# A 64-expert MoE layer: from four ranked experts per iteration to 48 pairs of 64-place tiles

## The reference

```python
def _moe(x, w_router, router_bias, w_gu, w_down, w_sh_gu, w_sh_down):
    scores = jax.nn.sigmoid((xt @ w_router).astype(jnp.float32))
    _, sel = lax.top_k(scores + router_bias.astype(jnp.float32), TOP_K)
    s_sel = jnp.take_along_axis(scores, sel, axis=-1)
    g = s_sel / jnp.sum(s_sel, axis=-1, keepdims=True) * ROUTED_SCALE
    gates_t = ...                                # 0 where a token is not routed
    def add_expert(e, acc):
        h = xt @ w_gu[e]
        a = jax.nn.silu(h[:, :D_EXPERT]) * h[:, D_EXPERT:]
        return acc + (a * gates_t[e][:, None]) @ w_down[e]
    routed = lax.fori_loop(0, N_EXPERTS, add_expert, jnp.zeros_like(xt))
    ...                                          # plus a shared expert of the same size
```

## Time and profile before

| | us |
|---|---|
| median of 3 runs (1662.83, 1664.14, 1669.38) | 1664.14 |
| the profiled execution, its span | 1662.2 |
| expert stage, layer 0: first B matmul to the layer norm's first add | 181.99 to 822.39 |
| expert stage, layer 1 | 1003.76 to 1647.36 |
| PE busy | 1594.4 (96%) |
| DVE, ACT, POOL busy | 900.1, 757.8, 438.0 |

### The profile page before, as it was taken

How to read it: one execution, slowest core, us unless ns; L and a number is a source line. 1 busy time by engine, 2 the same in 40 slices (tenths; PEclk the granted TensorE clock), 3 DMA queues, 4 the chain that set the end, 5 groups by cost and what they waited for, 6 DMA issues and landing times.

```text
span 1662.2 us, 28154 instructions
## 1 busy us (share of the span) xinstructions
PE 1594.4 (96%) x9726; PEld 1206.1 (73%) x9726; DVE 900.1 (54%) x1397; ACT 757.8 (46%) x1023; POOL 438.0 (26%) x307
## 2 busy tenths in 40 slices
PE   7999999999999999999899989999999999999996
PEld 7888776776767776777588876777776777766763
DVE  1876555445455555555648654555555555555446
ACT  5674344444444444444257643444444444444442
POOL 6671112221111222112266611111222112121230
PEclk9999999999999999999999999999999999999998
DMA  9542899999999999999873449999999999999993
GB/s 317 163 148 82 337 378 362 382 375 385 366 370 368 380 371 370 369 376 369 306 240 105 127 153 348 377 364 383 367 385 367 371 365 380 368 379 373 372 364 143
DMA packets 132948, 536.26 MB, mean 323 GB/s; under 512 B 22780, under 2 KB 62248, under 8 KB 82984
## 3 DMA queue, kind: packets, MB, share of 16 engines
q1 hardware_dynamic: 105648, 454.00, 69.4%
q0 software_dynamic: 23136, 76.60, 17.2%
q10 hardware_dynamic: 4120, 5.07, 1.0%
HBM read 495.60 MB, written 40.02 MB: 322 GB/s over the span
## 4 chain that ended last, share of the span: by engine, by line
PE 64%; DMA 14%; DVE 9%; ACT 4%; issue 4%; DVEq 4%; POOL 1%; ACTq 0%; SPq 0%; POOLq 0%
PE ps L1168 11%; DMA raw<-in_w_exp_down_dram 10%; PE ps L1070 10%; PE ps L1230 6%; PE ps L1048 5%; PE ps L1049 5%; PE ps L1050 5%; PE ps L804 5%; PE ps L1194 4%; PE ps L1078 4%; DVEq L1964 3%; ACT w_hi L1532 3%; DVE raw_r L1901 2%; PE ps L964 2%; DMA raw<-in_w_exp_gu_dram 2%
## 5 line engine op out<-in xcount | busy, mean ns | idle before, releaser
L1901 DVE TENSOR_TENSOR raw_r<-raw,w_hi 128x2048 fp32r<-128x2048 f32 x192 | 439.0, 2291 | 473.9 <-ACT w_hi L1532 473.8
L1532 ACT CAST w_hi<-raw 128x2048 fp32r<-128x2048 f32 x192 | 365.4, 1906 | 364.0 <-DMA raw<-in_w_exp_down_dram 222.4
L1048 PE MATMUL ps<-x_hi,w_hi 128*128 128x256 f32 x1072 | 306.9, 286 | 0.0
L1049 PE MATMUL ps<-x_lo,w_hi 128*128 128x256 f32 x1072 | 305.2, 285 | 0.0
L1050 PE MATMUL ps<-x_hi,raw_r 128*128 128x256 f32 x1072 | 303.2, 283 | 0.0
L1194 PE MATMUL ps<-raw,xc 128*64 128x512 f32 x1024 | 233.8, 598 | 1.2 <-DMA raw<-in_w_exp_gu_dram 1.2
L1048 PEld LDWEIGHTS ps<-x_hi,w_hi 128*128 128x128 f32 x1072 | 210.9, 197 | 28.6 <-issue 26.7
L1049 PEld LDWEIGHTS ps<-x_lo,w_hi 128*128 128x128 f32 x1072 | 212.5, 198 | 0.9
L1050 PEld LDWEIGHTS ps<-x_hi,raw_r 128*128 128x128 f32 x1072 | 212.7, 198 | 0.0
L1194 PEld LDWEIGHTS ps<-raw,xc 128*64 128x64 f32 x1024 | 67.8, 136 | 118.9 <-issue 109.6
L760 POOL DMA_INDIRECT sums_by_token<-o_c,token_out_c x30 | 74.1, 2469 | 291.9 <-DMA sums_by_token<-o_b,token_out 271.9
(11 more groups left out here) (359 smaller groups left out, 2819.0 us busy)
## 6 DMA issues: line engine op xcount, KB each, us to landing
raw<-in_w_exp_gu_dram SPq DMA_DIRECT2D x256, 1024.0 KB, 9.4
raw<-in_w_exp_down_dram SPq DMA_DIRECT2D x128, 1024.0 KB, 7.8
raw<-in_w_in_dram SPq DMA_DIRECT2D x22, 1024.0 KB, 10.3
raw<-in_w_out_dram SPq DMA_DIRECT2D x8, 1024.0 KB, 5.2
sums_by_token<-zeros POOLq DMA_DIRECT2D x10, 512.0 KB, 6.6
raw<-in_w_sh_gu_dram SPq DMA_DIRECT2D x4, 1024.0 KB, 5.2
row_a<-gates_by_rank SPq DMA_DIRECT2D x32, 128.0 KB, 11.7
raw<-in_w_in_dram SPq DMA_DIRECT2D x2, 1040.0 KB, 12.4
```

Of the source, the lines that this page charges most:

```text
L1048: nc.tensor.matmul(o, h, x_hi[:, c, :], start=(first and i == 0), stop=False, skip_group_check=True)
L1049: nc.tensor.matmul(o, h, x_lo[:, c, :], start=False, stop=False, skip_group_check=True)
L1532: nc.scalar.copy(w_hi[CAST[j] % 3][:], raw[:, j % RING, 0:UNIT_F]).then_inc(hi_done, 1)
L1901: nc.vector.tensor_tensor(raw_r[:, s, 0:UNIT_F], raw[:, s, 0:UNIT_F], w_hi[CAST[j] % 3][:], ALU.subtract)\
```

## The change

The expert stage becomes 48 pairs per layer. A pair is two tiles of 64 places side by side in plain fp32, as C1 and C2 were. 32 "base" pairs hold experts 2m and 2m+1, in fixed order; 16 "over" pairs stand for what does not fit into an expert's first 64 places. The list goes base, base, over, and again. The two tiles of an over pair fetch their weights by row index, a row outside the table's bounds being skipped; which tiles are in use is worked out from the counts on the chip. All 16 over pairs run through PE whether they hold anything or not.

- **PE**: per pair 16 matmuls of gate/up (L1176), 8 of the pair before's down (L1199), two transposes (L1186). The split weights and three-fold matmuls of A and B are gone, with the casts on ACT and the subtractions on DVE.
- **POOL**: per pair four gathers of token quarters (L699, 128 rows of 1 KB each), a read of the 128 places' sums (L711), a write of them (L718), and in two pairs of three a fetch of two over tiles' weights (L740 gate/up or L749 down). The read for pair n waits until the sums of pair n-2 are stored; the write of pair n-1 waits for DVE's addition. There are four sum tables in DRAM (two by parity, two by half), cleared in each layer.
- **DVE**: per pair it turns the gathered tokens (L1825, 128x1024), multiplies silu, gate and up (L1833) and adds PE's result to the sums read (L1842, two of 128x512). The last two pairs are not written back but added by a one-hot matmul; then the tables are read and added.
- **SP**: base weights only, six units per base pair, into 12 units (the ring of six and six more); a load waits for the base pair before last.
- **Routing part**: the ranking is gone. Per token and expert a code (column and place) is worked out; two sets of 16 matmuls turn them into a token index and a gate per place, and one more spreads the index over the four quarters.
- **Program's start**: POOL no longer waits for rows of zeros to land before it goes on; some 50 small constants (`table_at`) are set there.

```diff
+    NBASE = NE // 2
+    NOVER = (SEQ * TOPK // HALF - 1 + 1) // 2
+    NPAIR = NBASE + NOVER
+    KINDS = [("base", 2 * i + r) if r < 2 else ("over", i) for i in range(NOVER) for r in range(3)]
...
-                def gather(it, first=False):
...
-                with pool.Fori(0, NIT - 1) as it:
-                    gather(it + 1)
-                    pool.wait_ge(o_b_ready, done(layer, o_b_ready, it + 1))
-                    pool.sem_inc(pool_turn, 1)
-                    pool.indirect_dma_start(added_rows, bass.IndirectOffsetOnAxis(ap=token_out[:, 0:1], axis=0), o_b[:], None,
-                                            compute_op=ALU.add).then_inc(o_b_added, 16)
...
+                def fetch_x(n):
+
+                    for g in range(PIECES):
+                        pool.indirect_dma_start(xg[n % 2][:, g, :], None, x_rows,
+                                                bass.IndirectOffsetOnAxis(ap=x_at[:, g, COLUMN[n]:COLUMN[n] + 1], axis=0),
+                                                bounds_check=SEQ * PIECES - 1, oob_is_err=False).then_inc(xg_loaded[n % 2], 16)
...
+                for n in range(NADD + 1):
+                    if n + 2 < NPAIR:
+                        pool.wait_ge(xt_ready, done(layer, xt_ready, n + 1))
+                        pool.sem_inc(pool_turn, 1)
+                        fetch_x(n + 2)
+                    if 2 <= n:
+                        sums_landed(n - 2)
+                    if 1 <= n < NADD:
+                        fetch_sums(n)
+                    if n % 3 == 0 and n // 3 < NOVER:
+                        fetch_gate_up(n // 3)
+                    elif n % 3 == 1 and n // 3 < NOVER:
+                        fetch_down(n // 3)
+                    if n == NADD:
+                        fetch_tables(0)
+                    if n >= 1:
+                        store_sums(n - 1)
...
+                def gate_up(n):
+
+                    pe.wait_ge(xt_ready, done(layer, xt_ready, n + 1))
+                    if n >= 2:
+                        pe.wait_ge(act_ready, done(layer, act_ready, n - 1))
...
+                            for h in range(2):
+                                last = nc.tensor.matmul(ps[lane(h), n % 2, :], xt[n % 2][:, c, 2 * h:2 * h + 2, :].rearrange("p g s -> p (g s)"),
+                                                        gu_unit(n, h, half)[:, i, :], start=(c == 0), stop=(c == KC - 1))
...
+                for n in range(NPAIR):
+                    gate_up(n)
+                    if n >= 1:
+                        down(n - 1)
+                    transpose_act(n)
...
+                def add_sums(n):
+
+                    dve.wait_ge(sums_here[n % 2], done(layer, sums_here[n % 2], 16 * (n // 2 + 1)))
+                    for half in range(2):
+                        part = sums[n % 2][:, half * 512:(half + 1) * 512]
+                        dve.wait_ge(down_ps, done(layer, down_ps, 2 * n + half + 1))
+                        last = nc.vector.tensor_tensor(part, part, ps[:, 2 + 2 * (n % 2) + half, :], ALU.add)
+                    last.then_inc(sums_added, 1)
```

More of the change, by code:

```diff
@@ L227, in build @@
[L227 to L232, removed]
+        unit = [raw[:, s, 0:UNIT_F] for s in range(RING)]
+        unit += [sb(f"unit{RING + s}", [P, UNIT_F], where=[shared_base + s * KB8])[:] for s in range(RING)]
@@ L1138, in _ @@
[L1138 to L1142 removed]
+                pe.wait_ge(token_in_ready, done(layer, token_in_ready, 1))
+                for i in range(NT * TOPK):
+                    last = nc.tensor.matmul(ps[:, 2, 0:NPAIR], at_place[:, i, :], token_in[:, i, :], start=(i == 0),
+                                            stop=(i == NT * TOPK - 1))
@@ L1144, in _ @@
+                for i in range(NT * TOPK):
+                    last = nc.tensor.matmul(ps[:, 3, 0:NPAIR], at_place[:, i, :], gate_in[:, i, :], start=(i == 0),
+                                            stop=(i == NT * TOPK - 1))
+                last.then_inc(gate_ps, 1)
                 pe.wait_ge(a_ready, done(layer, a_ready, 1))
@@ L1263, in _ @@
-                with pe.Fori(0, NIT - 1) as it:
-                    step(it, False)
-                step(NIT - 1, True)
+                            for h in range(2):
+                                last = nc.tensor.matmul(ps[lane(h), 2 + 2 * (n % 2) + half, :], at_c[n % 2][:, c, lane(h)],
+                                                        down_unit(n, h)[:, c, half * 512:(half + 1) * 512],
+                                                        start=(c == 0), stop=(c == FC - 1))
+                        last.then_inc(down_ps, 1)
@@ new lines, in _ @@
+                dve.drain()
+                for t in range(NT):
+                    part = slice(t * TOPK, (t + 1) * TOPK)
+                    last = nc.vector.tensor_scalar(token_in[:, part, :], in_col[:, part, :], token_neg[:, t:t + 1], None, ALU.mult)
+                last.then_inc(token_in_ready, 1)
+                shared_lo(2)
+                dve.wait_ge(token_ps, done(layer, token_ps, 1))
+                nc.vector.tensor_scalar(token_at[:], ps[:, 2, 0:NPAIR], float(FAR), None, ALU.add)
@@ new lines, in add_tables @@
+                def add_tables(parity, t):
+                    dve.wait_ge(table_loaded[parity][t], done(layer, table_loaded[parity][t], 32))
+                    for h in range(2):
+                        dve.drain()
+                        last = nc.vector.tensor_tensor(x_tok[:, t, :], x_tok[:, t, :], tables[2 * parity + h][:, t * D:(t + 1) * D], ALU.add)
+                    return last
+                over_rows()
+                transpose_x_of(0)
+                dve.wait_ge(gate_ps, done(layer, gate_ps, 1))
@@ new lines, in _ @@
+                nc.vector.tensor_copy(gate_at[:], ps[:, 3, 0:NPAIR])
+                dve.drain()
+                dve.wait_ge(unit_used, done(layer, unit_used, SH))
+                dve.wait_ge(x_perm_ready, done(layer, x_perm_ready, NT))
+                for t in range(NT):
+                    for half in range(2):
+                        part = x_tok[:, t, half * 512:(half + 1) * 512]
+                        last = nc.vector.scalar_tensor_tensor(part, part, ALPHA, ps[:, 4 + 2 * t + half, :], ALU.mult, ALU.add)
```

991 lines of the change are left out of this document (414 added, 577 removed).

## The result

The changed kernel takes 1715.17 us (1710.06 to 1717.55) against 1663.49 for the kernel before in the same series: 1.029 times as long, interval 1.027 to 1.032. The forecast was 1539, faster.

| us | before | after | difference | forecast |
|---|---|---|---|---|
| start of layer 0 to first gate/up | 181.99 | 202.33 | +20.3 | +12.5 |
| expert stage, layer 0 | 640.4 | 647.3 | +6.9 | -72 |
| its end to layer 1's first gate/up | 181.4 | 202.5 | +21.2 | +10.5 |
| expert stage, layer 1 | 643.6 | 647.3 | +3.7 | -76 |

The account below looks back on a forecast made before the run. It took the DMA engines to bound the expert stage, closely followed by PE and POOL's chain: 1662.2 + 2 + 2 x 10.5 + (568 - 640.4) + (568 - 643.6) = 1537, as median 1539 us; own range 1493 to 1591.

Parts of the forecast that it names:

- the third price of the stage: Expert stage: POOL's chain of landings and issues takes 31.1 to 35.7 us per three pairs, just below the DMA engines.
- 2L + 14.9: POOL's chain per three pairs: two write landings L, each 8.1 to 10.4 us, plus issues of 6.2 and 8.7 us.
- The first rival: Expert stage: POOL's chain sets the period; 1607 us at landings of 11.1, 1650 at 11.8; chance 0.16.
- The second loop: Expert stage: read landing, addition, write landing for every two pairs, 23.6 us against 22.4 of PE.
- the routing part: Before the first gate/up in each layer: the new path adds 10.5 us per layer, 7 to 14.
- PE: a pair's gate/up: Expert stage: gate/up 7.16 us, down 3.58, 11.18 per pair with transposes, 33.5 per three pairs.
- The DMA engines: 35.7 forecast: Expert stage: transfers per three pairs need 35.7 us, bounds 34.4 and 37.8, the later limit than PE.
- the 568 forecast: Expert stage of each layer: 560 us by the DMA engines plus 8 for close limits; range 545 to 594.
- The start: Program's start: POOL's 9.92 us wait for zeros goes, constants take about as long; +2 us, from -5 to +5.
- The next layer's first weights: Between layers: they wait for the tables' addition, covered by the layer norm; if not, 10 us once.
- An issue of the new kinds: POOL, expert stage: rival that issuing sets the period, slower than before above 1.77 us per issue with gap; chance 0.13.
- Memory: Expert stage: rival that memory gives only 358 GB/s, stage 618 us, kernel 1639 us; chance 0.05.

Follow-up runs that it names:

- e4: The changed kernel without the fetches of over weights, except the first pair's; PE still runs all over pairs: 1578.63 us (one run).
- e3: The changed kernel with two thirds of the base weights' bytes left out, one chunk of each unit standing for all: 1479.1 us (one run).
- e1: The changed kernel with POOL's list reordered, over fetch and write of sums ahead of the landing wait and the read of sums: 1718.29 us.
- e8: The changed kernel with PE's two waits in the routing part filled by 22 and 5 matmuls that nobody reads: 1699.34 us.
- e5: e2 with PE's two waits in the routing part filled by 22 and 10 matmuls that nobody reads: 1557.76 us.
- e2: The changed kernel with the write of sums accumulating in the transfer and no read of sums; DVE copies instead of adding: 1565.68 us.
- e7: e2 without the fetches of over weights, except the first pair's: 1560.57 us (one run).

## Why the prediction was wrong

*The step that failed is the third price of the stage, POOL's chain.* The prediction set it at 31.1 to 35.7 us per three pairs, "Below the DMA engines, if only just", and so priced the stage by the DMA engines. It is 40.6, where the DMA engines need about 36 (e4), and so it set the period. In the formula 2L + 14.9 both terms were too low. The two landings were put at 16.2 to 20.8; by the medians they are 23.0. One of them, 9.8, lies in the forecast range of 8.1 to 10.4. The other, 13.2, does not: its write is queued behind two skipped fetches, of which the prediction counted the issues alone, and without them it lands after 10.6 (e4). Half the rows and no accumulation did not save the 2.3 us that the lower bound took off 10.4: beside full DMA engines such writes land after 10.6 and 9.6 (e4). What does shorten a landing is less traffic beside it (e3). And the rest is 17.3, not 14.9: an issue is 1.30 with its gap, not 1.24, and POOL goes on 0.8 us after a landing.

*The first rival had it.* It was priced at 1607 us for L of 11.1 and 1650 for 11.8, with a chance of 0.16. With the measured landings and rest it gives 23.0 + 17.3 = 40.3, close to the 40.6 of the trace; 16 x 40.6 = 650 for the stage's 647. Its 11.1 was near the mean of the two landings, 11.5; of the 3.5 us per three pairs that its price lacked, 2.4 lie in the rest. The second loop that it mentions, read, addition, write, is no footnote: e1 shows that it is just as long.

*The other step that failed is the routing part*: +10.5 per layer forecast; measured +20.3, of which 0.7 is the start, and +21.2. The operations and their order came out as written: codes done at 167.2 (166.3 forecast), token operands at 171.4 (170.4). But every matmul of the path was priced at full clock. Behind PE's idle 4.8 us it had half: tokens 6.88 for 3.6. Behind a second idle stretch of 4.4 us the gates took 7.06 for 3.6, and DVE's work on the gates was later by what the tokens delayed. With both stretches filled the first gate/up comes at 193.6 (e8). The earlier trace rows showed the same part of the old kernel with its own 24 records of the down matmul taking 7.4 us, 172.23 to 179.63 (the prediction read 7.2); e5's take 5.66. I had read that as a price, and not as a sign.

*What held.* PE: a pair's gate/up takes 7.04 and its down 3.46 (7.16 and 3.58 forecast), and with landings short (e3) PE is the limit. The DMA engines: 35.7 forecast, 35.6 and 36.3 in e4, which moves the forecast's bytes and whose stage takes 578.5 and 578.7 us for the 568 forecast. In e2 three pairs take 35.3 and 35.9; that its stage ends up within 8 us of the 568 holds for another design, since an accumulating write stands there for a read and a write, 34.6 by the prediction's own prices. Over pairs moved nothing. The start came out at +0.7 for +2 (the last operation on the mask of experts starts at 160.7 for 160.0). The next layer's first weights were covered: layer 1's part grew by 0.9 more than layer 0's.

*The other rivals.* An issue of the new kinds costs 1.30, far from the 1.77 at which issuing would have made the kernel slower; the right side for the wrong mechanism. Memory gave 387 GB/s in e2 over 480 us, beside the 358 that the Trainium skill ("HBM Reference", Specifications) gives as a core's effective share; the same section's remark that a lone core measures above it agrees with this row. The Trainium skill's fit for a transfer from POOL's queue ("DMA: Bandwidth & Descriptors", Anatomy of one DMA — SWDGE (gpsimd) path), by which 0.26 MB should land in an estimated 2.6 us, does not hold here: such writes landed after 13.2 and 9.8 us with all of the weight stream beside them, after 7.8 and 5.0 with a third of its bytes.

## What to carry to other kernels

A transfer that must land before the next one may be issued has to be priced as a loop: landing, issues in between, landing, with the landing taken from a stretch in which the other queues are as full as the new kernel will make them. Where a loop has a landing per step, changing the order exchanges one landing for another (e1); taking the dependence out, here by accumulating in the transfer, is what helps (e2). An empty transfer takes almost none of the DMA engines' time (e7), but it costs the engine that issues it an issue, and what is queued behind it can land later (e4). And a path that makes TensorE wait for small work of another engine should be priced at both levels of its clock.

## What was not expected of the hardware

- The same write of sums, 0.26 MB on average, landed after 13.2 or 7.8 us, and in its other place in the list after 9.8 or 5.0, by whether all of the weight stream or a third of its bytes ran beside it (e3). A write that moves nothing landed after 2.1 us while the weights stood still and after 9.0 beside full DMA engines (e4).
- An accumulating write needed no more time to land than a plain one: 10.1 and 10.0 us for the two base pairs in e7, 10.6 and 9.6 in e4, both without over fetches and beside full DMA engines.
- A fetch with all 128 rows out of bounds took POOL 0.99 us and a gap of 0.30, like a gather that moves data (1.02 and 0.30), and two of them held back the landing of the write behind them by 2.6 us (e4).
- Filling PE's two waits in the routing part, 4.8 and 4.4 us in a layer, with matmuls that nobody reads shortened the kernel by 16 us in two layers (e8).
